# The forgetting bias of an attention stage, moved from TensorE to a broadcast by DMA and the vector engine

## The chip, the cores and the metric

One core of one Trainium2 chip runs the whole program. The metric is the device time of one execution in microseconds (us), as a median over runs. All data is float32 (f32) in memory.

## The reference, cut to what matters

The program computes two transformer blocks over 256 tokens of width 2048: a first block (modulation vectors, a Fourier mixer, a squared-relu MLP) and a second block. The second block projects the normed tokens with one wide matrix `w_in` into queries, keys, values and gates of three mixers (gated linear attention, forgetting attention "fox" with 4 heads of 128, attention to a memory with 4 heads of 128), norms and gates their outputs, multiplies by `w_out`, and ends with another MLP. The change is in the logits of the forgetting attention:

```python
c = jnp.cumsum(log_f.astype(jnp.float32), axis=-1)          # (B, 4 heads, 256)
logits = (jnp.einsum('bhqd,bhkd->bhqk', qb, kb).astype(jnp.float32) * scale
          + c[:, :, q0:q1, None] - c[:, :, None, :q1])
mask = (q0 + jnp.arange(FOX_BLOCK))[:, None] >= jnp.arange(q1)[None, :]
p = jax.nn.softmax(jnp.where(mask, logits, -jnp.inf), axis=-1)
```

## The kernel before, in words

Every large weight matrix streams from memory once, in chunks of 512 KB (two 128-row slices by 512 columns) into a ring of 8 slots of `raw`. ScalarE copies a chunk to a rounded high half `wh` (L892), VectorE subtracts to make the low half `wl` (L1224, the function `lo`), and TensorE multiplies the halves with the high and low halves of the activations in 24 (or 12 wide) matmuls a chunk. One group is 8 chunks and makes 512 output columns; the second block's input projection is the 12 groups of `WIN_GROUPS`, numbered k = 0 to 11 (k = 4, 5, 6 are the fox queries, keys and values, k = 7 the memory queries, k = 8 to 11 the gates).

Each engine runs its own instruction list in order, and semaphores tie the lists together. The attention work is placed by hand between chunks of the projection. On TensorE the loop near the end of the tensor program calls it after chunk i of group k. The ones that matter here, by (k, i): after (7, 7) the sums of squares for the head norms; after (8, 3) `att_qk("fox", ...)` (L769), the logits, which go into PSUM banks 4 to 7; after (9, 0) `att_turn` (L787), which transposes the probabilities and waits for the semaphore `fox_p`; after (9, 4) `att_pv` (L795), which waits for `fox_pt`. The same three steps of the memory attention stand after (10, 3), (11, 2) and (11, 5).

In `att_qk` a float32 matmul shows as two records in the trace. For each of 4 heads and 2 query blocks there is one 128-row matmul of queries and keys (L774). For fox two more follow into the same PSUM region: the cumulated logarithms `fc` (4 partitions, 32 to 35, by 256 tokens) as stationary operand against a one-hot column `sel` (L777, gives +c of the query), and a row of minus one `nsel` against `fc` (L779, gives -c of the key). Both have 4 rows only. `sel` and `nsel` are loaded as constants.

On VectorE group k starts with `lo_run`, the low halves of chunks 4 to 7 of group k and 0 to 3 of group k + 1, so it runs ahead of TensorE by half a group. After it, at the end of k = 7, come the head norms of the fox queries and keys (`scale_heads`, L1613), which release the logits on TensorE (`fox_qk_ready`). After the `lo_run` of k = 8 comes `soft("fox", ...)`: it waits for the logits, adds the causal mask from PSUM to `pf` (L1651), takes the maximum (L1655), lets ScalarE exponentiate (L1135), and divides (L1660), which sets `fox_p`. ScalarE then goes on with the gates of group 8 (L1147 and on), and VectorE copies the transposed probabilities to `pt` (L1692).

GpSimd's list issues side DMAs: the mask and `nsel`, the spill of `h`, the reload of the memory keys and values `mk`, `mv`, and later the reload of `h`. `fc` is ready when the scan at L1760 ends, in group 0. In this stage slots 8 to 11 of `raw` are unused.

Of the kernel before, what the change touches and what calls it, by code (L numbers as in the profile page):

```python
# [34 lines left out]
P = 128  # L35
D = 2048
S = 256
# [31 lines left out]

def program(nc, x, c, w_mod, b_mod, norm_g, w_mlp_in, w_mlp_out, fnet_w_out, mem, attn_g, w_in, gla_w2, gla_b,  # L70
            fox_b, fox_qg, fox_kg, mem_g, w_mem_kv, mem_qg, mem_kg, out_g, w_out, mlp_g, w_up, w_down,
            k_ident, k_dft, k_mask, k_nsel, k_sel, k_levels, out):
    ctx = ExitStack()
    with ctx:
        sems = {}
# [69 lines left out]
        mk = at("mk", [P, 4, S], F32, O_ACC1)  # L145
        mv = at("mv", [P, HALVES, GC], F32, O_ACC1 + 4 * KB)
        mask = at("mask", [P, HALVES, S], F32, O_SLOT)
        nsel = at("nsel", [64, 4, P], F32, O_SLOT + 2 * KB)

        ident = const("ident", [P, P], F32)  # L150
        ones = const("ones", [P, P], F32)
        vrow = const("vrow", [P, P], F32)
        vt = const("vt", [P, VROWS], F32)
        lmask = const("lmask", [P, 8, P], U8, 1)
        sel = const("sel", [64, 4], F32)
        foxb = const("foxb", [64, 1], F32)
        eps = const("eps", [P, 1], F32)
        silu32 = const("silu32", [P, KT, QP], F32)
# [7 lines left out]
        ps = ctx.enter_context(nc.psum_tensor("ps", [P, 8, 512], F32))  # L166
        mk_dram = nc.dram_tensor("mk_spill", [P, 4 * S], F32).ap()
        mv_dram = nc.dram_tensor("mv_spill", [P, HALVES * GC], F32).ap()
        h_dram = nc.dram_tensor("h_spill", [P, HALVES * D], F32).ap()

        def rows(w):
# [2 lines left out]
        def flat(ap):  # L174
            return ap.rearrange("p a b -> p (a b)")
# [175 lines left out]
        def _(pool):  # L351
# [56 lines left out]

            pool.wait_ge(sem("slot_used"), 4 + MODN)
            pool.dma_start(mask[:, :, :], k_mask.rearrange("p (a s) -> p a s", a=HALVES)).then_inc(sem("att_const"), 16)  # L410
            pool.dma_start(nsel[32:36, :, :], k_nsel.rearrange("p (a s) -> p a s", a=4)).then_inc(sem("att_const"), 16)
            pool.wait_ge(sem("h_piece"), 8)
            pool.dma_start(h_dram, flat(h[:, :, :])).then_inc(sem("h_spilled"), 16)
            pool.wait_ge(sem("la_mm"), 1)
# [3 lines left out]
            pool.wait_ge(sem("mv_spilled"), 16)  # L418
            pool.dma_start(flat(mk[:, :, :]), mk_dram).then_inc(sem("mkv_in"), 16)
            pool.dma_start(flat(mv[:, :, :]), mv_dram).then_inc(sem("mkv_in"), 16)  # L420
            pool.wait_ge(sem("mem_pv"), 1)
            pool.wait_ge(sem("h_spilled"), 16)
            pool.dma_start(flat(h[:, :, :]), h_dram).then_inc(sem("h_back"), 16)
# [3 lines left out]
        def _(pe):  # L427
# [338 lines left out]
                    last = mm(ps[:, bank + j, :], ones[:, :], flat(sq[:, 2 * j:2 * j + 2, :]), start=True, stop=True)  # L766
                last.then_inc(sem(name + "_mm"), 1)

            def att_qk(name, qq, kk, fox):  # L769
                pe.wait_ge(sem(name + "_qk_ready"), 1)  # L770
                for hd in range(4):
                    for tb in range(HALVES):
                        o = ps[:, 4 + hd, tb * S:(tb + 1) * S]
                        last = mm(o, qq[:, hd, tb * P:(tb + 1) * P], kk[:, hd, :], start=tb == 0, stop=not fox,  # L774
                                  skip_group_check=True)
                        if fox:
                            mm(o, fc[32:36, tb * P:(tb + 1) * P], sel[32:36, hd:hd + 1].to_broadcast([4, S]),  # L777
                               start=False, stop=False, skip_group_check=True)
                            last = mm(o, nsel[32:36, hd, :], fc[32:36, :], start=False, stop=True, skip_group_check=True)  # L779
                last.then_inc(sem(name + "_qk"), 1)  # L780

            def att_turn(name, pr):
# [17 lines left out]
            for k, (name, off) in enumerate(WIN_GROUPS):  # L800
                G = G_WIN + k
                bank_free(G)
                for i in range(CH):
                    if k == 0 and i % 2 == 0:
                        pe.wait_ge(sem("xt_ready"), 8 + i // 2 + 1)
                    sr = (i, CH * G + i + 1)
                    if name in ("gv", "fv"):
                        N_chunk(G, i, xt, False, *sr)
                    else:
                        T_chunk(G, i, False, *sr)  # L810
                    if (k, i) == (0, 1):
                        att_narrow()
                    if (k, i) == (0, 5):
                        att_la()
                    if 2 <= k <= 6 and i == 3:
                        att_level(2 * (k - 2))
                    if 2 <= k <= 5 and i == 6:
                        att_level(2 * (k - 2) + 1)
                    if (k, i) == (6, 6):
                        att_gla_out()  # L820
                    if (k, i) == (7, 3):
                        att_sums("o", 1, osq, 8, 4)
                    if (k, i) == (7, 7):
                        pe.wait_ge(sem("o_ln"), 1)
                        att_sums("fq", 1, fqsq, 4, 4)
                        att_sums("fk", 1, fksq, 4, 6)
                    if (k, i) == (8, 3):
                        pe.wait_ge(sem("att_const"), 32)
                        att_qk("fox", fq, fk, True)
                    if (k, i) == (9, 0):  # L830
                        att_turn("fox", pf)
                    if (k, i) == (9, 4):
                        att_pv("fox", lambda sb_, hd: fvv[:, sb_, hd * P:(hd + 1) * P])
                        att_sums("mq", 1, tmp, 4, 6)
                    if (k, i) == (9, 7):
                        att_sums("fo", 1, fosq, 4, 4)
                    if (k, i) == (10, 3):
                        pe.wait_ge(sem("mkv_in"), 32)
                        pe.wait_ge(sem("fo_ln"), 1)
                        att_qk("mem", mq, mk, False)  # L840
                    if (k, i) == (11, 2):
                        att_turn("mem", pm)
                    if (k, i) == (11, 5):
                        att_pv("mem", lambda sb_, hd: mv[:, sb_, hd * P:(hd + 1) * P])
                    if (k, i) == (11, 7):
                        att_sums("mo", 1, tmp, 4, 6)
# [30 lines left out]
        def _(act):  # L877
            A = nc.scalar.activation
            col = lambda t: t.rearrange("(a o) -> a o", o=1)
            consts = [(dft_raw[:, :, :], k_dft.rearrange("(a p) n -> p a n", p=P)),  # L880
                      (foxb[32:36, :], col(fox_b)), (sel[32:36, :], k_sel), (lmask_raw[:, :], k_levels)]
            assert len(consts) == N_CONSTS
            row_loads(act, 0)
            for dst, src in consts:
# [326 lines left out]
        def _(dve):  # L1211
# [434 lines left out]
            def soft(name, pr, masked):  # L1646
# [1 line left out]
                dve.wait_ge(sem(name + "_qk"), 1)  # L1648
                src, dst = ps[:, 4:8, :], banks(pr[:, :, :], 4)
                if masked:  # L1650
                    link(V.tensor_tensor(dst, src, flat(mask[:, :, :]).rearrange("p (o n) -> p o n", o=1)  # L1651
                                         .to_broadcast([P, 4, 2 * S]), ALU.add))
                else:
                    link(V.tensor_copy(dst, src))
                link(V.tensor_reduce(mx[:, :], pr[:, :, :], AX.X, ALU.max))  # L1655
# [42 lines left out]
            for k, (name, off) in enumerate(WIN_GROUPS):  # L1698
# [73 lines left out]
                if k == 7:  # L1772
                    dve.wait_ge(sem("fq_root"), 1)
                    dve.wait_ge(sem("fk_root"), 1)
                    link(scale_heads(fq, lambda j: v("fqg"), fqsq[:, :, :], 4))
                    scale_heads(fk, lambda j: v("fkg"), fksq[:, :, :], 4).then_inc(sem("fox_qk_ready"), 1)

            for g in range(GQ):
                G = G_WO + g
# [14 lines left out]
WIN_GROUPS = [("gq", 0), ("gk", 0), ("gv", 0), ("gv", GC), ("fq", 0), ("fk", 0), ("fv", 0), ("mq", 0),  # L1794
              ("gg", 0), ("gg", GC), ("fg", 0), ("mg", 0)]
N_ROWS = 13
N_CONSTS = 4
G1_ROWS_AT = {0: 8, 1: 12, 3: 16, 5: 24, 6: 28}
G1_AT = [(6, 7), (), (), (20, 21), (22, 23), (), (), ()]

# [5 lines left out]
def shape_constants():  # L1806
# [9 lines left out]
        "k_ident": np.eye(P, dtype=np.float32),  # L1816
        "k_dft": np.concatenate([np.cos(angle), np.sin(angle)], 1).astype(np.float32),
        "k_mask": np.concatenate(causal, 1).astype(np.float32),
        "k_nsel": np.repeat(-np.eye(4, dtype=np.float32), P, axis=1),
        "k_sel": np.eye(4, dtype=np.float32),  # L1820
        "k_levels": np.concatenate(masks, 1).astype(np.float32),
    }

# [17 lines left out]
```

## Time and profile before

| | |
|---|---|
| median of 3 runs | 2235.99 us (2235.28 to 2237.89) |
| the profiled execution | 2238.09 us, its span 2236.3 us |
| TensorE busy (PE) | 2155.4 us |
| VectorE busy (DVE) | 1317.2 us |
| ScalarE busy (ACT) | 973.7 us |
| mean granted TensorE clock | 0.977 of full |

The span is the time from the first to the last instruction on the core. A granted clock of 1.00 is TensorE's full 2.4 GHz and 0.50 is 1.2 GHz. Matmuls are pipelined, so the busy time of TensorE also counts the overlap of neighbours and is no measure of throughput; the chain that ended last, and the distance from one matmul's step in it to the next, show the pace. Idle time of an engine that nobody waits for costs nothing.

### The profile page before, as it was taken

Reading aid. Unit: us, or ns where it says so; the run is one execution under the profiler, and the core shown is the slowest. Engines: PE = TensorE matmul, PEld = TensorE weight load, DVE = VectorE, ACT = ScalarE, POOL = GpSimd, SP = SyncE. Lnnn points to the kernel's source line nnn. Section 1 sums busy time; section 2 is a strip of 40 time slices with the busy share of each in tenths; the row PEclk is TensorE's granted clock in tenths of the full one; section 3 lists DMA queues with packets and bytes.
Section 4 is the critical chain, followed back from the end, with each engine's and each line's share of the span. In section 5 each row is a group of like instructions: output and inputs, shape, how many; then the busy total and the mean of one; then the engine's idle time right before and its main releaser. Section 6 shows DMA issues by size and latency. Waiting matters only on the chain.

```text
span 2236.3 us, 31309 instructions
## 1 busy us (share of the span) xinstructions
PE 2155.4 (96%) x11753; PEld 1823.1 (82%) x11753; DVE 1317.2 (59%) x1301; ACT 973.7 (44%) x1133; POOL 45.1 (2%) x69
## 2 busy tenths in 40 slices
PE   5999988999999999997999999999999999999999
PEld 3867867888888888886979879888888888888887
DVE  3568976555655555655666546646545554655563
ACT  4244435443444444443533447744444343443342
POOL 0000000000000000000000000000000000000000
PEclk9889989999999999998999989999999999999999
DMA  9899996667666667676455435556656656656654
GB/s 389 280 403 347 391 372 194 215 216 215 206 224 207 213 210 218 205 223 203 145 164 147 136 100 145 191 186 188 189 194 189 186 192 189 187 190 193 183 192 151
DMA packets 219188, 478.98 MB, mean 214 GB/s; under 512 B 14708, under 2 KB 15084, under 8 KB 218336
## 3 DMA queue, kind: packets, MB, share of 16 engines
q1 hardware_dynamic: 211940, 450.98, 62.5%
q0 software_dynamic: 6480, 25.69, 3.6%
q8 instruction: 60, 0.98, 0.2%
q10 hardware_dynamic: 684, 1.14, 0.1%
q14 instruction: 24, 0.20, 0.0%
HBM read 472.50 MB, written 5.24 MB: 214 GB/s over the span
## 4 chain that ended last, share of the span: by engine, by line
PE 88%; DVE 5%; DMA 4%; ACT 2%; issue 1%; SPq 0%; DVEq 0%; ACTq 0%
PE ps L441 21%; PE ps L459 13%; PE ps L461 13%; PE ps L460 13%; PE ps L442 11%; PE ps L445 3%; PE ps L446 3%; PE ps L447 3%; DMA raw<-in_w_mod_dram 1%; DVE acc L1249 1%; DMA raw<-in_w_in_dram 1%; PE ps L485 1%; PE ps L507 1%; DVE wl L1224 1%; DMA slot<-in_norm_g_dram 1%
## 5 line engine op out<-in xcount | busy, mean ns | idle before, releaser
L1224 DVE TENSOR_TENSOR wl<-raw,wh 128x1024 fp32r<-128x1024 f32 x688 | 811.2, 1220 | 345.5 <-ACT wh L892 344.4
L892 ACT ACTIVATE wh<-raw 128x1024 fp32r<-128x1024 f32 x688 | 700.7, 1054 | 559.0 <-DMA raw<-in_w_down_dram 161.6
L441 PE MATMUL ps<-xt,wh 128*128 128x512 f32 x2048 | 724.8, 399 | 9.0 <-DVE wl L1224 9.0
L442 PE MATMUL ps<-xt,wl 128*128 128x256 f32 x2048 | 575.5, 281 | 0.0
L441 PEld LDWEIGHTS ps<-xt,wh 128*128 128x128 f32 x2048 | 386.2, 189 | 106.1 <-issue 10.7
L459 PE MATMUL ps<-wh,u 128*128 128x512 f32 x1152 | 449.3, 390 | 0.0
L460 PE MATMUL ps<-wl,u 128*128 128x512 f32 x1152 | 448.2, 389 | 0.0
L461 PE MATMUL ps<-wh,u 128*128 128x512 f32 x1152 | 448.2, 389 | 0.0
L442 PEld LDWEIGHTS ps<-xt,wl 128*128 128x128 f32 x2048 | 388.3, 190 | 0.3
L459 PEld LDWEIGHTS ps<-wh,u 128*128 128x128 f32 x1152 | 216.2, 188 | 45.2 <-issue 0.5
L461 PEld LDWEIGHTS ps<-wh,u 128*128 128x128 f32 x1152 | 216.2, 188 | 45.1
L460 PEld LDWEIGHTS ps<-wl,u 128*128 128x128 f32 x1152 | 216.2, 188 | 44.9 <-issue 0.5
L445 PE MATMUL ps<-xt,wh 128*128 128x256 f32 x640 | 187.6, 293 | 4.0 <-DVE wl L1224 4.0
L446 PE MATMUL ps<-xt,wh 128*128 128x256 f32 x640 | 184.2, 288 | 0.0
L447 PE MATMUL ps<-xt,wl 128*128 128x256 f32 x640 | 184.1, 288 | 0.0
L1502 DVE TENSOR_TENSOR tmp<-ps,tmp 128x1024 f32<-128x1024 f32 x32 | 39.2, 1225 | 172.7 <-ACT tmp L1067 172.7
L445 PEld LDWEIGHTS ps<-xt,wh 128*128 128x128 f32 x640 | 126.1, 197 | 9.1 <-issue 8.5
L446 PEld LDWEIGHTS ps<-xt,wh 128*128 128x128 f32 x640 | 126.1, 197 | 1.1 <-issue 1.0
L447 PEld LDWEIGHTS ps<-xt,wl 128*128 128x128 f32 x640 | 126.0, 197 | 0.0
L1067 ACT ACTIVATE tmp<-ps 128x1024 f32<-128x1024 f32 x32 | 32.9, 1027 | 201.1 <-PE ps L442 201.1
L459 PE MATMUL ps<-wh,xt 128*128 128x512 f32 x256 | 102.5, 400 | 3.6 <-DVE wl L1224 3.6
L1249 DVE SCALAR_TENSOR_TENSOR acc<-raw,siluc,acc 128x1024 f32<-128x1024 f32 x80 | 102.2, 1279 | 4.9 <-DMA raw<-in_w_mod_dram 1.7
(266 smaller groups left out, 1514.5 us busy)
## 6 DMA issues: line engine op xcount, KB each, us to landing
raw<-in_w_mod_dram SPq DMA_DIRECT2D x160, 512.0 KB, 8.0
raw<-in_w_mlp_in_dram SPq DMA_DIRECT2D x128, 512.0 KB, 3.8
raw<-in_w_mlp_out_dram SPq DMA_DIRECT2D x128, 512.0 KB, 3.9
raw<-in_w_up_dram SPq DMA_DIRECT2D x128, 512.0 KB, 3.8
raw<-in_w_down_dram SPq DMA_DIRECT2D x128, 512.0 KB, 3.7
raw<-in_w_in_dram SPq DMA_DIRECT2D x96, 512.0 KB, 3.7
raw<-in_fnet_w_out_dram SPq DMA_DIRECT2D x32, 512.0 KB, 5.6
slot<-in_w_mod_dram POOLq DMA_DIRECT2D x32, 512.0 KB, 4.6
```

Of the source, the lines that this page charges most:

```text
L441: mm(o, a, flat(xt[:, kt, :, :]), start=first, stop=end, skip_group_check=True)
L442: last = mm(o[:, 0:S], b, xt[:, kt, 0, :], start=False, stop=end, skip_group_check=True)
L445: mm(o, a, xt[:, kt, 0, :], start=first and j % 2 == 0, stop=False, skip_group_check=True)
L446: mm(o, a, xt[:, kt, 1, :], start=False, stop=False, skip_group_check=True)
L447: last = mm(o, b, xt[:, kt, 0, :], start=False, stop=end, skip_group_check=True)
L459: mm(o, hi, wh[:, i, t, :], start=kt == 0, stop=False, skip_group_check=True)
L460: mm(o, hi, wl[:, s, t, :], start=False, stop=False, skip_group_check=True)
L461: last = mm(o, lo, wh[:, i, t, :], start=False, stop=kt == KT - 1, skip_group_check=True)
L892: A(flat(wh[:, i, :, :]), raw[:, landed[0], :], ACT.Copy).then_inc(sem("w_hi"), 1)
L1224: V.tensor_tensor(flat(wl[:, s, :, :]), raw[:, s, :], flat(wh[:, i, :, :]).bitcast(F32), ALU.subtract).then_inc(sem("w_lo"), 1)
L1249: V.scalar_tensor_tensor(out=t, in0=raw[:, s, :], scalar=siluc[:, kt:kt + 1], in1=t, op0=ALU.mult, op1=ALU.add).then_inc(mod_used(mod_c(c0 ...
L1502: V.tensor_tensor(tmp[:, :, :], ps[:, b0:b0 + 4, 0:S], tmp[:, :, :], ALU.add).then_inc(sem("evacuated"), 1)
```

## The change: what it does

The 32 calls of four-row matmuls (L777, L779) go; `att_qk` keeps its 8 query-key matmuls. In their place `fc` is written to memory by GpSimd's queue, and read back twice: broadcast to all 128 partitions (`fcb`, 4 heads by 256 keys, 512 KB), and with queries on partitions (`fcq`, 128 by 8 numbers, 4 bytes each). VectorE then makes `bias` = mask + fcq - fcb in 8 instructions of 128x256 at the end of group k = 7, behind the instruction that releases the logits on TensorE and ahead of the `lo_run` of k = 8. `soft` adds `bias` where it added the mask. The constants `sel` and `nsel` and their loads go.

```diff
+        fcq = at("fcq", [P, 8], F32, O_SLOT + 3 * KB)
+        fcb = at("fcb", [P, 4, S], F32, O_RAW + RAW * 4 * KB + 4 * KB)
+        bias = at("bias", [P, 8, S], F32, O_RAW + RAW * 4 * KB + 8 * KB)
...
             pool.dma_start(flat(mv[:, :, :]), mv_dram).then_inc(sem("mkv_in"), 16)
+            pool.wait_ge(sem("fc_ready"), 1)
+            pool.dma_start(fc_dram, fc[32:36, :]).then_inc(sem("fc_out"), 16)
+            pool.wait_ge(sem("fc_out"), 16)
+            pool.dma_start(flat(fcb[:, :, :]), fc_dram.rearrange("h s -> (h s)").rearrange("(o n) -> o n", o=1)
+                           .to_broadcast([P, 4 * S])).then_inc(sem("fc_in"), 16)
+            pool.dma_start(fcq[:, :].rearrange("p (h t) -> p h t", h=4),
+                           fc_dram.rearrange("h (t p) -> p h t", p=P), allow_slow_non_contiguous=True).then_inc(sem("fc_in"), 16)
             pool.wait_ge(sem("mem_pv"), 1)
...
-                        last = mm(o, qq[:, hd, tb * P:(tb + 1) * P], kk[:, hd, :], start=tb == 0, stop=not fox,
-                                  skip_group_check=True)
-                        if fox:
-                            mm(o, fc[32:36, tb * P:(tb + 1) * P], sel[32:36, hd:hd + 1].to_broadcast([4, S]),
-                               start=False, stop=False, skip_group_check=True)
-                            last = mm(o, nsel[32:36, hd, :], fc[32:36, :], start=False, stop=True, skip_group_check=True)
+                        last = mm(ps[:, 4 + hd, tb * S:(tb + 1) * S], qq[:, hd, tb * P:(tb + 1) * P], kk[:, hd, :],
+                                  start=tb == 0, stop=True, skip_group_check=True)
...
-                    link(V.tensor_tensor(dst, src, flat(mask[:, :, :]).rearrange("p (o n) -> p o n", o=1)
-                                         .to_broadcast([P, 4, 2 * S]), ALU.add))
+                    link(V.tensor_tensor(dst, src, banks(bias[:, :, :], 4), ALU.add))
...
                     scale_heads(fk, lambda j: v("fkg"), fksq[:, :, :], 4).then_inc(sem("fox_qk_ready"), 1)
+                    dve.wait_ge(sem("att_const"), 16)
+                    dve.wait_ge(sem("fc_in"), 32)
+                    for j in range(8):
+                        last = V.scalar_tensor_tensor(out=bias[:, j, :], in0=mask[:, j % 2, :], scalar=fcq[:, j:j + 1],
+                                                      in1=fcb[:, j // 2, :], op0=ALU.add, op1=ALU.subtract)
+                    link(last)
```

## Rows read from the trace of the kernel before

**Rows 1.** The page: an engine's busy time, and shares of the chain that ended last.

```profile
PE 2155.4 (96%) x11753; PEld 1823.1 (82%) x11753; DVE 1317.2 (59%) x1301; ACT 973.7 (44%) x1133; POOL 45.1 (2%) x69
...
PE 88%; DVE 5%; DMA 4%; ACT 2%; issue 1%; SPq 0%; DVEq 0%; ACTq 0%
```

**Rows 2.** Windows: stretch, length, busy by engine, granted clock, DMA share, GB/s.

```profile
1307.65:1312.35 4.70, 4.70 (x18) 2.61 (x17) 4.70 (x5) 2.11 (x2) 0.00 (x0) 1.00 0.42 122
1312.35:1328.36 16.01, 16.01 (x32) 8.39 (x31) 2.10 (x2) 0.00 (x0) 0.00 (x0) 0.50 0.00 0
1328.36:1332.90 4.54, 4.54 (x22) 4.54 (x23) 4.47 (x2) 0.00 (x0) 0.00 (x0) 0.51 0.00 0
1332.90:1344.91 12.01, 12.01 (x103) 12.01 (x102) 2.67 (x11) 6.86 (x19) 0.00 (x0) 1.00 0.63 169
1385.24:1388.70 3.46, 3.46 (x19) 3.04 (x18) 2.74 (x3) 1.86 (x3) 0.00 (x0) 1.00 0.59 175
```

**Rows 3.** Chain that ended last, TensorE: start, length, line, records.

```profile
1307.65 0.43 PE ps L774 x2
...
1309.14 0.63 PE ps L774 x2
...
1322.05 1.15 PE ps L774 x2
...
1325.20 1.15 PE ps L774 x2
...
1327.50 0.85 PE ps L779 x2
...
1344.91 1.75 PE ps L787 x16
```

**Rows 4.** VectorE in order of time: start, length, line; idle before, releaser.

```profile
1289.18 3.26 DVE L1613 SCALAR_TENSOR_TENSOR ot<-ot,vt,osq 128x256 f32<-128x256 f32 x8 [5.28 <-ACT osq L1130]
...
1305.28 9.16 DVE L1224 TENSOR_TENSOR wl<-raw,wh 128x1024 fp32r<-128x1024 f32 x8
1328.39 2.29 DVE L1651 TENSOR_TENSOR pf<-ps,mask 128x2048 f32<-128x2048 f32 x1 [13.95 <-PE ps L779]
...
1337.56 2.19 DVE L1660 TENSOR_SCALAR pf<-pf,rs 128x256 f32<-128x256 f32 x8
...
1355.61 2.28 DVE L1692 COPY pt<-ps 128x2048 f32<-128x2048 f32 x1
```

**Rows 5.** ScalarE in order of time: the last exponential's read-out, the gate after it.

```profile
1337.11 0.19 ACT L1135 ACTIVATION_READ_ACCUMULATOR pf<-pf,nmx 128x1 f32 x1
1342.07 1.02 ACT L1147 ACTIVATE gt<-ps 128x1024 f32<-128x1024 f32 x1 [4.77 <-PE ps L447]
```

**Rows 6.** Waits from 1405 to 1412 us: total, times, longest.

```profile
PE ps L787 <- DVE pm L1660: 0.6, 1, 0.6
```

**Rows 7.** Windows: TensorE idle, or the busy stretch right after.

```profile
176.90:180.44 3.54, 0.02 (x2) 0.00 (x1) 3.47 (x11) 2.18 (x5) 0.00 (x0) 0.81 1.02 400
180.44:185.46 5.02, 5.02 (x23) 5.02 (x24) 4.92 (x9) 0.00 (x0) 0.00 (x0) 0.50 0.95 342
66.88:70.84 3.96, 0.00 (x0) 0.03 (x1) 3.78 (x4) 0.38 (x1) 0.00 (x0) 0.88 0.72 227
70.84:76.66 5.82, 5.82 (x27) 5.82 (x28) 2.93 (x3) 1.06 (x1) 0.00 (x0) 0.50 0.99 340
...
1172.14:1173.97 1.83, 0.00 (x1) 0.00 (x1) 1.29 (x2) 0.45 (x1) 0.00 (x0) 1.00 0.64 142
...
305.95:307.60 1.65, 0.00 (x1) 0.00 (x0) 0.00 (x0) 1.57 (x4) 0.00 (x0) 1.00 1.01 387
```

**Rows 8.** VectorE in order of time: the end of the scan, the copy in group 1.

```profile
1107.56 0.47 DVE L1760 TENSOR_TENSOR_SCAN fc<-ones,fc,fft 4x128 f32<-4x128 f32 x1
...
1123.98 1.22 DVE L1744 COPY kg<-ps 128x1024 f32<-128x1024 f32 x1 [5.42 <-PE ps L447]
```

**Rows 9.** DMA issues, 1000 to 1020 us: form, size, median us to landing.

```profile
wsr<-in_w_in_dram POOLq DMA_DIRECT2D x1, 128.0 KB, 6.3
```

More of the change, by code:

```diff
@@ L71, in program @@
             fox_b, fox_qg, fox_kg, mem_g, w_mem_kv, mem_qg, mem_kg, out_g, w_out, mlp_g, w_up, w_down,
-            k_ident, k_dft, k_mask, k_nsel, k_sel, k_levels, out):
+            k_ident, k_dft, k_mask, k_levels, out):
     ctx = ExitStack()
@@ L147, in program @@
         mask = at("mask", [P, HALVES, S], F32, O_SLOT)
-        nsel = at("nsel", [64, 4, P], F32, O_SLOT + 2 * KB)
+        fcq = at("fcq", [P, 8], F32, O_SLOT + 3 * KB)
+        fcb = at("fcb", [P, 4, S], F32, O_RAW + RAW * 4 * KB + 4 * KB)
+        bias = at("bias", [P, 8, S], F32, O_RAW + RAW * 4 * KB + 8 * KB)
         ident = const("ident", [P, P], F32)
@@ L154, in program @@
         lmask = const("lmask", [P, 8, P], U8, 1)
-        sel = const("sel", [64, 4], F32)
         foxb = const("foxb", [64, 1], F32)
@@ L168, in program @@
         mv_dram = nc.dram_tensor("mv_spill", [P, HALVES * GC], F32).ap()
+        fc_dram = nc.dram_tensor("fc_spill", [4, S], F32).ap()
         h_dram = nc.dram_tensor("h_spill", [P, HALVES * D], F32).ap()
@@ L410, in _ @@
             pool.dma_start(mask[:, :, :], k_mask.rearrange("p (a s) -> p a s", a=HALVES)).then_inc(sem("att_const"), 16)
-            pool.dma_start(nsel[32:36, :, :], k_nsel.rearrange("p (a s) -> p a s", a=4)).then_inc(sem("att_const"), 16)
             pool.wait_ge(sem("h_piece"), 8)
@@ L767, in att_sums, with att_qk @@
                 last.then_inc(sem(name + "_mm"), 1)
-            def att_qk(name, qq, kk, fox):
+            def att_qk(name, qq, kk):
                 pe.wait_ge(sem(name + "_qk_ready"), 1)
@@ L772, in att_qk @@
                     for tb in range(HALVES):
-                        o = ps[:, 4 + hd, tb * S:(tb + 1) * S]
-                        last = mm(o, qq[:, hd, tb * P:(tb + 1) * P], kk[:, hd, :], start=tb == 0, stop=not fox,
-                                  skip_group_check=True)
-                        if fox:
-                            mm(o, fc[32:36, tb * P:(tb + 1) * P], sel[32:36, hd:hd + 1].to_broadcast([4, S]),
-                               start=False, stop=False, skip_group_check=True)
-                            last = mm(o, nsel[32:36, hd, :], fc[32:36, :], start=False, stop=True, skip_group_check=True)
+                        last = mm(ps[:, 4 + hd, tb * S:(tb + 1) * S], qq[:, hd, tb * P:(tb + 1) * P], kk[:, hd, :],
+                                  start=tb == 0, stop=True, skip_group_check=True)
                 last.then_inc(sem(name + "_qk"), 1)
@@ L827, in _ @@
                     if (k, i) == (8, 3):
-                        pe.wait_ge(sem("att_const"), 32)
-                        att_qk("fox", fq, fk, True)
+                        att_qk("fox", fq, fk)
                     if (k, i) == (9, 0):
@@ L839, in _ @@
                         pe.wait_ge(sem("fo_ln"), 1)
-                        att_qk("mem", mq, mk, False)
+                        att_qk("mem", mq, mk)
                     if (k, i) == (11, 2):
@@ L880, in _ @@
             consts = [(dft_raw[:, :, :], k_dft.rearrange("(a p) n -> p a n", p=P)),
-                      (foxb[32:36, :], col(fox_b)), (sel[32:36, :], k_sel), (lmask_raw[:, :], k_levels)]
+                      (foxb[32:36, :], col(fox_b)), (lmask_raw[:, :], k_levels)]
             assert len(consts) == N_CONSTS
@@ L1796 @@
 N_ROWS = 13
-N_CONSTS = 4
+N_CONSTS = 3
 G1_ROWS_AT = {0: 8, 1: 12, 3: 16, 5: 24, 6: 28}
@@ L1818, in shape_constants @@
         "k_mask": np.concatenate(causal, 1).astype(np.float32),
-        "k_nsel": np.repeat(-np.eye(4, dtype=np.float32), P, axis=1),
-        "k_sel": np.eye(4, dtype=np.float32),
         "k_levels": np.concatenate(masks, 1).astype(np.float32),
```

## The prediction

> **What bounds the kernel now.** I read the page first. TensorE is busy 96% of the span and 88% of the chain that ended last is TensorE's, while the vector engine is busy 59% [rows 1]. A cut of TensorE work is worth its length, as long as nobody else becomes late. So the second view is the chain around the changed block, and the third is the windows cut at its borders.
>
> The fox logits take TensorE from 1307.65 us to 1328.36 (the last piece of L779 starts at 1327.50 and takes 0.85) [rows 3], so 20.7 us. The memory attention's logits are the same 8 matmuls without the 32 four-row ones and take 3.46 us at full clock [rows 2]. The reader should see two causes in the 20.7. First, the round of three matmuls repeats every 1.49 us at the start (1307.65 to 1309.14), where a lone query-key pair would take 3.46 / 8 = 0.43. Second, from the fourth round on it repeats every 3.15 us (1322.05 to 1325.20) [rows 3]: the granted clock is 1.00 up to 1312.35 and 0.50 from there, that is 1.2 instead of 2.4 GHz [rows 2]. The engine had issued matmuls without a gap since the block began, two thirds of them with 4 rows. The clock stays low for 4.54 us after the block: five chunks of 24 matmuls stand between the block and the transpose, 21 of these 120 steps take 4.54 us and the 99 others 12.01, which is 0.12 each [rows 2]. All 120 at full clock would be 14.4 us. So the block costs 20.7 + 2.0 (4.54 less 21 x 0.12 = 2.5), against 3.46 without the four-row matmuls: **19.3 us** less for TensorE alone.
>
> A rule of the Trainium skill speaks against that size. "TensorE: Matmul & The Clock Gate", in the part on LDWEIGHTS of "Part 2: What happens when you issue a matmul", says that time goes by columns and the row count does not matter. By that the 48 records of 256 columns would take 48 / 16 x 3.46 = 10.4 us and the cut would be 6.9 us; the trace has 20.7, so it does not agree, at either clock. The sum goes by the trace.
>
> **The vector engine's side.** Before, it had nothing to do for 13.95 us ahead of the mask addition, waiting for L779 [rows 4]. That slack goes, and what stands behind it must be walked through. Times are those of the profiled execution; everything up to 1305.28 stays.
> - At 1305.28 the release of the logits has been given, and `lo_run` of k = 8 starts, 8 instructions in 9.16 us [rows 4]. The change puts its 8 bias instructions ahead. The same operation on 128x256 with the same operand kinds took 3.26 us for 8 (L1613) [rows 4]; this one I take at 3.3. Nothing hides it, since the engine has no gap from there to the softmax. `lo_run` runs from 1308.6 to 1317.7.
> - Queued behind them on the engine are the low halves that TensorE wants. The first, chunk (8, 4), is ready at 1308.6 + 1.2 = 1309.8. TensorE wants it when the logits end, at 1307.65 + 3.46 = 1311.1. It is in time by 1.3 us, and the others gain on it, for a chunk takes 24 x 0.12 = 2.9 us on TensorE and 1.15 on the vector engine.
> - The softmax starts at 1317.7 instead of 1328.39. From the start of the addition to the end of the division it took 1337.56 + 2.19 - 1328.39 = 11.36 us [rows 4], ScalarE's part included; the addition of `bias` has the shape and the PSUM source of that of the mask, so I take it the same. `fox_p` comes at 1329.1.
> - TensorE does five chunks between the logits and the transpose: 1311.1 + 14.4, with 0.3 for the switch of matmul kinds, is 1325.8. Then **it waits 3.3 us**, for `fox_p`. The transpose starts at 1329.15 instead of 1344.91 [rows 3]: **15.8 us** earlier. The other 3.5 of the 19.3 are the bias instructions, come back as a wait. That such a chain can be late shows in the memory attention, where the transpose has two chunks (5.8 us) more of cover and TensorE still waits 0.6 us [rows 6].
> - The wait has a price in clock. After idle stretches of 3.54 and 3.96 us TensorE's clock had fallen inside the stretch (means of 0.81 and 0.88), and it stood at 0.50 for 5.02 and 5.82 us of work afterwards; an idle of 1.83 us did nothing [rows 7]. At 305.95, 1.65 us of idle showed 1.00. A wait of 3.3 us is nearest to the first. Priced: the transpose, 1.75 us at full clock [rows 3], takes twice that, as the round of the logits did (3.15 against 1.49), +1.75; the other 1.5 us of a 5.0 us slow stretch lose 1.5 x (1 - 0.120 / 0.216) = 0.65, with 4.54 / 21 = 0.216 for the slow step [rows 2]. Together **+2.4 us**. Bounds: 0 if the clock holds; 2.75 for a stretch of 5.8 us.
> - What is late next: `att_pv` wants `pt`. ScalarE ends its exponentials 8.9 us after the addition starts (1337.3) and then waited 4.77 us for group 8 to end before the gate at 1342.07 [rows 5]. Now it goes straight on, at 1317.7 + 8.9 = 1326.7, 15.4 earlier. The copy to `pt` ended at 1357.9 [rows 4], so now at 1342.5. TensorE gets there at 1329.15 + 1.75 + 4 chunks = 1342.4, or 1344.8 with the slow clock. So 0 to 0.1 us. The rest of the program follows TensorE's pace as it did, and shifts as a whole.
>
> **The DMAs.** `fc` is ready at 1108.0 [rows 8], and `fcq`, `fcb` are needed at 1305.3, 197 us later. GpSimd's queue has nothing behind them but the reload of `h`, which waits for the memory attention (after 1420). The only price is in the way of the weight ring at 1110 to 1120. There the vector engine waits 5.42 us before its copy at 1123.98 [rows 8], so weights that are late by less cost nothing. `fcb` is 512 KB, like one weight chunk. `fcq` is 1024 runs of 4 bytes; the nearest row is `wsr`, 2048 runs of 64 bytes, landed in 6.3 us among other loads [rows 9]. I take 0, with 3 us as the upper bound (half of `wsr`'s time with the ring standing still). The two small constant loads that go were never waited for: between 0 and 0.3 us of gain, taken as 0.
>
> **The sum.** 19.3 - 3.5 - 2.4 = 13.4 us less. Against the profiled execution, 2238.09 - 13.4 = 2224.7; that execution was 2.1 us over the median of 2235.99, so the time on the median is **2222.6 us**.
>
> **The rivals.**
> 1. The wait comes, but the clock holds, as in the idle stretches of 1.83 and 1.65 us: 15.8 less, **2220.2**. For it: 3.3 us is shorter than both stretches that ended slow. A variant gives the same time: if the clock fell at 1312 from whatever cause, and not from the four-row matmuls, TensorE would come to the transpose 2 us later and the wait would swallow it. Against the variant: the memory logits kept 1.00 [rows 2]. Chance 0.25.
> 2. The clock falls and stays low for long, since transposes of 128 columns may do less to lift it than full matmuls. With 10 us low the loss is 1.75 + 6.5 x 0.44 = 4.6: **2224.8**. Chance 0.08.
> 3. The cover holds: the softmax is not what TensorE waits for, and all 19.3 come: **2216.7**. Against it stands the length of the chain above, each link with a row. Chance 0.03.
> 4. The gain is eaten to less than 4.5 us: bias instructions at 1.2 us each instead of 0.41 (the copy of four times the elements took 1.22 [rows 8]) add 8 x 0.8 = 6.3 us of wait, and up to 4 more if the low halves then come late too: 13.4 - 6.3 = 7.1 down to 3, **2229 to 2233**. Chance 0.04.
> 5. Slower than before: the 1024 four-byte runs choke the 16 DMA engines at 1110 to 1120. It decides from the point where the ring stands still for more than the 5.42 us of slack plus the 13.4 gained, so 19 us, and gives over **2236**. That is 0.3 us per run on one engine (19 x 16 / 1024); `wsr`, with twice the runs, took 6.3 us in all, under 0.05 each. Chance 0.02. The Trainium skill, "DMA: Bandwidth & Descriptors", "Specifications", has a read-modify-write below 512 bytes a run, which speaks for such a price but gives no number for it here.
>
> **How the numbers follow.** The forecast has 0.58. The range goes from 2218 (rival 1 with 2 us for what the execution-to-execution spread of 2.6 us allows) to 2228.5 (rival 2, plus 3 us of DMA, plus 0.7), which leaves out rivals 3, 5 and most of 4. Within 0.2% is within 4.5 us of 2235.99, about what a measurement of this kernel can tell from no change: chance 0.04, from rival 4 at its dearest and mishaps in the DMA; slower 0.02; faster 0.94.
>
> **What would show it.** Right: the logits as 16 records of L774's form in about 3.5 us at clock 1.00; 8 bias instructions of about 0.41 us; no idle of the vector engine before the addition; TensorE waiting about 3.3 us at the transpose for L1660's counterpart, and 0.50 in the 5 us after it; the transpose 21.5 us after the first logit matmul, where it was 37.3 (1307.65 to 1344.91) [rows 3]. Wrong: an idle vector engine before the addition (cover longer than I think), a wait at `fc_in`, ScalarE waiting for weights at 1110 to 1125, or a new wait at `att_pv`.

## The result, and the profile after

The changed kernel takes 2222.5 us (median of 4 runs, 2221.3 to 2224.6), where the kernel before takes 2236.94 (4 runs, 2235.28 to 2241.51): a ratio of 0.9938, with a 95% interval of 0.9925 to 0.9952. That is 14.4 us less. The profiled execution took 2221.78 us, its span 2219.8.

One number ahead of the prediction, and in it, wants a correction: the change removes 16 calls of four-row matmuls, not 32. Each call is two records, so there are 32 records, and every duration in the prediction was taken by records or by pieces of the chain.

The page of the changed kernel, busy times and shares of the chain that ended last (compare [rows 1]):

```profile
PE 2136.3 (96%) x11721; PEld 1811.5 (82%) x11721; DVE 1320.7 (59%) x1309; ACT 973.4 (44%) x1133; POOL 46.5 (2%) x71
...
PE 86%; DVE 6%; DMA 4%; ACT 3%; issue 1%; SPq 0%; DVEq 0%; ACTq 0%
```

TensorE has 32 records less, the vector engine 8 instructions more, and the vector engine's share of the chain has risen. Why it has is in the chain itself, from the changed kernel's trace (start, length, line, records):

```profile
1302.92 3.18 DVE bias L1781 x8
...
1306.12 9.17 DVE wl L1226 x8
1315.30 2.21 DVE pf L1653
...
1320.06 4.06 ACT pf L1137 x16
...
1324.38 2.20 DVE pf L1661 x8
...
1326.63 2.59 PE ps L790 x16
...
1341.66 3.46 PE ps L798 x16
```

From 1302.9 to 1326.6 the chain no longer runs through TensorE: bias instructions, low halves, softmax, then the transposes (L790). Before, TensorE's logits stood there [rows 3]. The vector engine's row for the addition has no idle time in it, where it had 13.95 us [rows 4]:

```profile
1315.22 2.28 DVE L1653 TENSOR_TENSOR pf<-ps,bias 128x2048 f32<-128x2048 f32 x1
```

In group 1, where the new DMAs run, the last low half and the copy behind it, first before, then after:

```profile
1117.34 1.23 DVE L1224 TENSOR_TENSOR wl<-raw,wh 128x1024 fp32r<-128x1024 f32 x1 [1.23 <-ACT wh L892]
```

```profile
1117.31 1.23 DVE L1226 TENSOR_TENSOR wl<-raw,wh 128x1024 fp32r<-128x1024 f32 x1 [3.63 <-ACT wh L894]
1121.56 1.23 DVE L1745 COPY kg<-ps 128x1024 f32<-128x1024 f32 x1 [3.02 <-PE ps L455]
```

The idle time ahead of the low half grew by 2.4 us and that ahead of the copy shrank by as much, from 5.42 us [rows 8]. The two together stay at 6.65 us. The low half waits for ScalarE, whose wait for this chunk of weights grew from 1.76 to 4.20 us.

Windows of the changed kernel: the logits, the wait, the stretch after it (columns as in [rows 2]), and the wait by name:

```profile
1305.20:1308.66 3.46, 3.46 (x19) 3.04 (x18) 3.42 (x6) 1.06 (x1) 0.00 (x0) 1.00 0.61 171
1323.05:1326.63 3.58, 0.01 (x2) 0.01 (x1) 2.39 (x9) 3.55 (x8) 0.00 (x0) 1.00 0.60 171
1326.63:1331.20 4.57, 4.57 (x27) 4.57 (x28) 2.97 (x3) 4.52 (x5) 0.00 (x0) 0.63 0.00 0
```

```profile
PE ps L790 <- DVE pf L1661: 3.6, 1, 3.6
```

The logits take 3.46 us at full clock. TensorE then waits 3.58 us for the probabilities. The clock holds in the wait and falls behind it: a mean of 0.63 over the 4.57 us that follow, at levels of 1.00 and 0.50.

A caution on comparing the two profiled executions. Their spans differ by 16.5 us. The end of the fox norms, which nothing of the change precedes but the DMAs and the two constant loads that went, stands at 1305.28 before (start of the next row in [rows 4]) and at 1302.84 after, 2.44 us apart. The same spot of the program comes between 1300.7 and 1306.2 us in the profiles of this study. So I measure from there. The kernel before has its product of probabilities and values at this place of its chain:

```profile
1358.17 3.50 PE ps L795 x16
```

That is 52.9 us behind the norms before, and 38.8 after (1341.66). It makes 14.1 us of gain by the change itself, and 2.4 us that were there when the norms ended.

### The profile page after: what moved, and what is told of

It is laid out like the page before. It is cut to its first block, busy times and chain, and to the rows that moved or that the text cites. A ratio compares the mean times of both kernels' runs of the same rounds, so it can differ in the third digit from the quotient of the medians.

```text
span 2219.8 us, 31255 instructions
## 1 busy us (share of the span) xinstructions
PE 2136.3 (96%) x11721; PEld 1811.5 (82%) x11721; DVE 1320.7 (59%) x1309; ACT 973.4 (44%) x1133; POOL 46.5 (2%) x71
## 4 chain that ended last, share of the span: by engine, by line
PE 86%; DVE 6%; DMA 4%; ACT 3%; issue 1%; SPq 0%; DVEq 0%; ACTq 0%
PE ps L449 21%; PE ps L467 13%; PE ps L468 13%; PE ps L469 13%; PE ps L450 11%; PE ps L453 3%; PE ps L455 3%; PE ps L454 3%; DMA raw<-in_w_mod_dram 1%; DVE acc L1251 1%; DVE wl L1226 1%; PE ps L493 1%; PE ps L515 1%; DMA raw<-in_w_in_dram 1%; DMA slot<-in_norm_g_dram 1%
```

## The experiments

Twelve runs follow, two of them repeats of a kernel, in three groups, each on one chip together with the kernel before (its medians there: 2236.2, 2236.5, 2236.3 us). The 95% intervals of the ratios reach about 3 us to either side, so the claims below lean on the traces, and the times check them. Where a distance "from the norms" is given, it runs from the end of the fox norms, as above.

**The bias instructions earlier.** They move into the vector engine's idle time ahead of the norms' roots.

```diff
                 if k == 7:
+                    dve.wait_ge(sem("att_const"), 16)
+                    dve.wait_ge(sem("fc_in"), 32)
+                    for j in range(8):
+                        last = V.scalar_tensor_tensor(out=bias[:, j, :], in0=mask[:, j % 2, :], scalar=fcq[:, j:j + 1],
+                                                      in1=fcb[:, j // 2, :], op0=ALU.add, op1=ALU.subtract)
+                    link(last)
                     dve.wait_ge(sem("fq_root"), 1)
                     dve.wait_ge(sem("fk_root"), 1)
                     link(scale_heads(fq, lambda j: v("fqg"), fqsq[:, :, :], 4))
                     scale_heads(fk, lambda j: v("fkg"), fksq[:, :, :], 4).then_inc(sem("fox_qk_ready"), 1)
-                    dve.wait_ge(sem("att_const"), 16)
-                    dve.wait_ge(sem("fc_in"), 32)
-                    for j in range(8):
...
-                    link(last)
```

> The changed kernel with its 8 bias instructions moved ahead of the wait for the norms' roots at the end of group 7, where the vector engine idles 7.9 us. Theory (the bias instructions stand on the chain to the softmax, and the 3.6 us wait that they make lowers TensorE's clock): the probabilities come 3.3 us earlier, TensorE waits about 0.3 us at the fox transpose, the clock stays at 1.00, and 3.3 + 1.8 = 5.1 us go: about 2217.4 us where the changed kernel has 2222.5. Rival (something else sets the wait, weights or ScalarE): the wait stays over 3 us and the time within 1 us of 2222.5.

Measured: 2219.35 us, ratio 0.9927 (0.9914 to 0.994). First the vector engine's row and the transposes and product in the chain, then TensorE's wait, all of this kernel:

```profile
1293.49 3.25 DVE L1777 SCALAR_TENSOR_TENSOR bias<-mask,fcq,fcb 128x256 f32<-128x256 f32 x8
```

```profile
1325.34 1.97 PE ps L790 x16
1338.82 3.49 PE ps L798 x16
```

```profile
PE ps L790 <- DVE pf L1661: 0.3, 1, 0.3
```

The wait falls from 3.6 to 0.3 us, as the theory has it. The product starts 34.0 us from the norms (1338.82 less 1304.85), 4.8 earlier than in the changed kernel's profile. The rival is out. The median fell by less than the expected 5.1; it was run again on a third chip:

> The kernel with the bias instructions ahead of the norms' wait once more, as footing for the next three on one chip. Theory: 2219.4 us, as on the first chip.

Measured: 2217.63 us, ratio 0.9916 (0.9902 to 0.9929), the product 34.0 us from the norms again.

**No bias at all.** The kernel leaves out the bias: no spill, no reloads, no bias instructions.

```diff
-            pool.wait_ge(sem("fc_ready"), 1)
-            pool.dma_start(fc_dram, fc[32:36, :]).then_inc(sem("fc_out"), 16)
...
-                    dve.wait_ge(sem("fc_in"), 32)
-                    for j in range(8):
...
-                    link(V.tensor_tensor(dst, src, banks(bias[:, :, :], 4), ALU.add))
+                    link(V.tensor_tensor(dst, src, flat(mask[:, :, :]).rearrange("p (o n) -> p o n", o=1)
+                                         .to_broadcast([P, 4, 2 * S]), ALU.add))
```

> The changed kernel without the forgetting bias at all: no spill of the cumulated logarithms, no reloads, no bias instructions, the mask alone is added; the output lacks the bias. Theory (the DMAs are free, the bias instructions cost only by their place): the same as the kernel with the bias instructions moved ahead, about 2217.4 us. Rival (the broadcast and the four-byte reload hold up the weight ring): over 1 us faster than that kernel, and ScalarE waits less for weights between 1105 and 1125 us.

Measured: 2218.91 us, ratio 0.992 (0.9906 to 0.9935). The chain of this kernel:

```profile
1326.41 1.97 PE ps L783 x16
...
1339.89 3.49 PE ps L791 x16
```

The product stands 34.0 us from the norms (1339.89 less 1305.91), like the kernel with the early bias instructions, and the times agree. One sign of the rival did show: without the DMAs ScalarE waits 1.78 us for the weights near 1117 us, where it waits 4.24 with them in the kernel with the early instructions. The time doesn't show it, because the vector engine's idle time behind takes it in. So the whole machinery of the bias, 3 DMAs and 8 instructions, costs nothing once the instructions sit in a gap, and its 3.3 us plus what the clock takes where the change puts them.

**128 rows in place of 4,** on the kernel before. Each four-row matmul becomes one more query-key matmul, so the bias is left out and the logits are wrong.

```diff
-                            mm(o, fc[32:36, tb * P:(tb + 1) * P], sel[32:36, hd:hd + 1].to_broadcast([4, S]),
+                            mm(o, qq[:, hd, tb * P:(tb + 1) * P], kk[:, hd, :],
                                start=False, stop=False, skip_group_check=True)
-                            last = mm(o, nsel[32:36, hd, :], fc[32:36, :], start=False, stop=True, skip_group_check=True)
+                            last = mm(o, qq[:, hd, tb * P:(tb + 1) * P], kk[:, hd, :], start=False, stop=True, skip_group_check=True)
```

> The kernel before with each of its 32 four-row matmuls replaced by one more 128-row query-key matmul into the same place (the output is not the reference's; the bias is left out). Theory (four rows lower the clock and break the pace): 48 records at 0.216 us, 10.4 us for the block, clock 1.00 through it and after it, about 12.3 us less than before: 2224.6 where before has 2236.9. Rival (the number of rows does not matter; any f32 block of this length lowers the clock): the block takes 20 us and the time is that of before.

Measured: 2224.73 us, ratio 0.9944 (0.993 to 0.9958). Chain and window of the block:

```profile
1307.96 0.43 PE ps L774 x2
1308.40 0.43 PE ps L777 x2
```

```profile
1307.96:1318.32 10.36, 10.36 (x51) 9.12 (x50) 6.80 (x6) 2.11 (x2) 0.00 (x0) 1.00 0.19 58
```

The block of 24 matmuls, now all with 128 rows, takes 10.4 us, where it took 20.7 with 16 of them at four rows [rows 3], and the clock stays at 1.00. The rival is out: a block of this length doesn't lower the clock by itself.

**32 rows in place of 4,** in the same place and order, the bias left out and the logits wrong (`qq[32:64, ...]`, `kk[32:64, ...]` in the lines above).

> The kernel before with its four-row matmuls replaced by matmuls of 32 rows of the queries and keys (partitions 32 to 63), in the old order; the bias is left out and the output is not the reference's. Theory (few rows are the cause, of the pace and of the clock): 32 rows behave nearly as 4 do, rounds of 1.5 us and a fall of the clock, the time within 3 us of before. Rival (only the very few rows count, or the operands' kind): rounds of 1.3 us and a clock at 1.00, as with 128 rows, 2224.7.

Measured: 2226.95 us, ratio 0.9962 (0.9949 to 0.9975). Both expectations missed a half. Chain and window:

```profile
1306.37 0.62 PE ps L777 x2
1306.99 0.43 PE ps L779 x2
1307.42 0.63 PE ps L774 x2
```

```profile
1305.93:1319.22 13.29, 13.29 (x50) 7.50 (x48) 6.80 (x6) 2.11 (x2) 0.00 (x0) 1.00 0.15 44
```

The pieces have the slow rhythm 0.62, 0.43, 0.63 of the four-row kernel (a round of 1.69), but the clock never falls. So the two costs are two things. The rhythm comes with the alternation of 128-row and short matmuls, at 4 rows and at 32 alike: 13.3 less 10.4 = 2.9 us. The clock falls with 4 rows and not with 32. The time agrees: 9.5 us under before, where the block is 7.4 us shorter and the 2.0 us of slow clock behind it are gone.

**The same four-row matmuls, grouped:** first the 8 query-key calls, then the 16 four-row calls.

```diff
+                for hd in range(4 if fox else 0):
+                    for tb in range(HALVES):
+                        o = ps[:, 4 + hd, tb * S:(tb + 1) * S]
+                        mm(o, fc[32:36, tb * P:(tb + 1) * P], sel[32:36, hd:hd + 1].to_broadcast([4, S]),
+                           start=False, stop=False, skip_group_check=True)
+                        last = mm(o, nsel[32:36, hd, :], fc[32:36, :], start=False, stop=True, skip_group_check=True)
```

> The kernel before with its matmuls in another order: first the 8 query-key matmuls, then all the four-row matmuls together; same work, same output. Theory (two causes: the switch between 128-row and four-row matmuls keeps the weight load from running ahead, and few rows lower the clock): no more 0.63 us pieces, one record each 0.216 us at full clock, but the clock still falls some 5 us into the block and the rest goes at 0.43: the block takes about 15.7 us where it took 20.7, and the time is 5 us under before, 2231. Rival (the alternation itself lowers the clock): the clock stays at 1.00, block 10.4 us, 12 us under before: 2224.

Measured: 2229.7 us (10 runs, 2224.9 to 2235.3), ratio 0.9974 (0.9962 to 0.9987), with 2227.09 for the profiled execution. Chain and windows:

```profile
1304.05 3.46 PE ps L774 x16
1307.50 0.63 PE ps L779 x2
1308.13 0.43 PE ps L781 x2
...
1312.61 0.85 PE ps L781 x2
```

```profile
1304.05:1312.20 8.15, 8.15 (x38) 6.78 (x38) 6.79 (x6) 2.11 (x2) 0.00 (x0) 1.00 0.26 72
1312.20:1322.50 10.30, 10.30 (x39) 8.81 (x38) 4.75 (x3) 0.73 (x3) 0.00 (x0) 0.50 0.01 2
```

One 0.63 remains, at the one switch; every other piece is 0.43 until the clock falls, 8.2 us into the block, 4.7 us into its four-row part. Before, it fell 4.7 us into a block that alternates from the start, 4.3 after its first four-row matmul [rows 2, 3]. The block takes 12.8 us. With no alternation left the clock falls still, so the alternation isn't its cause. What stays untested is whether the number of rows does it or what the rows hold: the four-row matmuls read the cumulated logarithms with a one-hot column or with rows of minus one, and their 32-row and 128-row substitutes read queries and keys. Four rows of queries and keys were not run. I expected the fall 5 us into the block, that is, earlier; hence 12.8 and not 15.7 in this execution. The spread of the runs (10.4 us, against 2 to 8 in the other kernels) fits a fall that comes at varying times, but only one execution was profiled.

**The transposes one chunk later,** in the changed kernel: `if (k, i) == (9, 1)` for `(9, 0)`.

> The changed kernel with the fox transpose one chunk later on TensorE, after (9, 1). Theory (the wait is a lack of cover, and its clock price goes with it): TensorE waits 0.7 us, clock 1.00, 2.9 + 1.8 = 4.7 us less: about 2217.8 us. Rival (the wait moves to the next step, the product of probabilities and values after (9, 4), whose operand the vector engine copies after the transpose): the time stays within 1 us of 2222.5.

Measured: 2222.84 us, ratio 0.9941 (0.9928 to 0.9954): the rival. One of its 6 runs took 9809 us, which nothing on record explains. It is in that median and not in the ratio; the median of the other five is 2222.31. TensorE's waits, and the window behind the one of 2.7 us:

```profile
PE ps L798 <- DVE pt L1693: 4.0, 2, 2.7
PE ps L790 <- DVE pf L1661: 0.7, 1, 0.7
```

```profile
1338.60:1345.00 6.40, 6.38 (x19) 4.89 (x20) 6.40 (x6) 2.52 (x3) 0.00 (x0) 0.73 0.07 26
```

(The 4.0 counts also the wait of about 1.4 us of the memory attention, which is in every profile but the last.) The clock fell behind this wait too, 1.4 us into the product. The transposes wait 0.7 us as expected, and the product 2.7: its operand comes from ScalarE's gate steps and the vector engine's copy, which run at their own pace from the end of the exponentials. Moving the transposes doesn't move that. My prediction had this number: it put the copy at 0 to 0.1 us behind TensorE, and I did not carry it into this expectation.

**The changed kernel again, with and without filling the wait.** In the second, 28 matmuls of full rows stand in the wait ahead of the transposes.

```diff
                     if (k, i) == (9, 0):
+                        pe.wait_ge(sem("fox_max"), 1)
+                        for n in range(28):
+                            mm(ps[:, 4, 0:S], xt[:, 0, 0, 0:P], xt[:, 0, 0, :], start=True, stop=True, skip_group_check=True)
                         att_turn("fox", pf)
```

> The changed kernel itself, on one chip with the next three, as their footing. All theories: 2222.5 us, 13 to 14 us under before.

> The changed kernel with 28 idle-filling matmuls (256 columns, high halves, into PSUM bank 4, which the transposes then overwrite) in TensorE's wait before the fox transpose; they wait for the softmax's maximum, so that the logits have been read. Theory (the idle lowers the clock, which costs 1.6 us): the clock stays at 1.00, transpose and the four chunks after it run at full pace, 1.6 us less than the changed kernel: 2220.9. Rival (the stretch after the transpose is slow for another reason, such as the f32 transposes themselves): the clock falls as before, and the time is that of the changed kernel or up to 0.5 us more.

Measured: 2222.17 us, ratio 0.9936 (0.9922 to 0.995), and 2221.45 us, ratio 0.9932 (0.9919 to 0.9946). The windows of the first, wait and after it, and where its product starts:

```profile
1323.10:1326.78 3.68, 0.12 (x2) 0.01 (x1) 2.40 (x9) 3.65 (x9) 0.00 (x0) 1.00 0.60 174
1326.78:1331.35 4.57, 4.57 (x40) 4.57 (x41) 2.97 (x3) 4.52 (x5) 0.00 (x0) 1.00 0.00 0
```

```profile
1340.25 3.49 PE ps L798 x16
```

The window after the wait, of the kernel with the filling:

```profile
1327.60:1341.10 13.50, 13.49 (x113) 13.49 (x114) 10.88 (x9) 11.84 (x12) 0.00 (x0) 1.00 0.41 112
```

The same kernel, the same wait of 3.6 us, and this time the clock held without any filling. From the start of the transposes to the product it takes 13.5 us here (1326.78 to 1340.25), where it took 15.0 in the first profile (1326.63 to 1341.66): the price of the fall, when it comes, is **1.6 us**. The filling gained 0.7 us in the median, within the scatter. As the clock held without it, this pair doesn't decide between its two expectations, and how often the clock falls isn't settled by it. Both traces of the filled and the unfilled kernel have the same distance to the product.

**The bias instructions twice,** in their place, the second time over the first.

> The changed kernel with the 8 bias instructions done twice in their place (same output). Theory (they stand one for one on the chain to the transposes, and a wait of this length always lowers the clock): TensorE waits 6.9 us at the fox transpose instead of 3.6, the clock falls in it, and the time is 3.3 us over the changed kernel where that one's clock fell too, 4.9 over where it held: 2225.5 to 2227. Rival (slack further on takes it back): under 1.5 us over 2222.2.

Measured: 2227.91 us, ratio 0.9963 (0.995 to 0.9976). TensorE's waits, the longer one being the later, then its clock around the earlier wait (1313 to 1319 us) and, in the last window, behind the later one (columns as in [rows 2]):

```profile
PE ps L790 <- DVE pf L1661: 3.1, 1, 3.1
PE ps L453 <- DVE wl L1226: 2.0, 1, 2.0
```

```profile
1313.00:1314.00 1.00, 0.00 (x0) 0.00 (x0) 1.00 (x2) 0.24 (x1) 0.00 (x0) 1.00 0.00 0
1314.00:1315.00 1.00, 1.00 (x7) 1.00 (x8) 1.00 (x1) 0.00 (x0) 0.00 (x0) 0.79 0.00 0
1315.00:1316.00 1.00, 1.00 (x6) 1.00 (x6) 1.00 (x2) 0.00 (x0) 0.00 (x0) 0.50 0.00 0
...
1317.00:1318.00 1.00, 1.00 (x7) 1.00 (x7) 1.00 (x2) 0.00 (x0) 0.00 (x0) 0.50 0.00 0
1318.00:1319.00 1.00, 1.00 (x10) 1.00 (x10) 1.00 (x2) 0.00 (x0) 0.00 (x0) 1.00 0.00 0
...
1333.00:1337.00 4.00, 3.77 (x33) 3.77 (x34) 2.34 (x3) 3.95 (x5) 0.00 (x0) 1.00 0.06 21
```

The 3.3 us go on the path one for one: the transposes start 3.3 us later from the norms (27.1 against 23.8), which rules out slack further on. I expected one wait of 6.9. There are two: the low half of chunk (8, 4), for which the prediction had counted 1.3 us of slack, is now late by 2.0 = 3.3 - 1.3. After that short wait the clock is at 0.50 for 3.4 us, at a loss of 3.4 x 0.44 = 1.5, which the second wait takes in: 2.0 + 1.5 + 3.1 = 6.6 of the 6.9. The second wait, longer than the first, leaves the clock at 1.00. That a wait of this length always lowers the clock, as I had assumed, is refuted. The median is 1 us above the range that I gave.

**The four-byte reload five times,** into four more buffers that nobody reads.

```diff
-            pool.dma_start(fcq[:, :].rearrange("p (h t) -> p h t", h=4),
+            for t in (fcq, *fcx):
+                pool.dma_start(t[:, :].rearrange("p (h t) -> p h t", h=4),
...
```

> The changed kernel with the four-byte reload done five times at once, into four more small buffers that nobody reads. In the profiles one set of reloads took the vector engine's idle time before its copy of group 1 from 5.4 to 3.0 us. Theory (1024 runs of 4 bytes hold the 16 DMA engines for under 1 us): the idle time falls by up to 1 us for each extra reload and stays at or over 0, and the time rises by under 1 us on 2222.2. Rival (the four-byte runs are what cost the 2.4 us): four more cost 9.6 us, of which the 3.0 us of idle time hide a part: about 6.6 us more, 2228.8.

Measured: 2221.55 us, ratio 0.9938 (0.9923 to 0.9954). DMA issues between 1100 and 1135 us, the vector engine's copy of group 1, and the window from the start of the fox transposes:

```profile
fcb<-fc_spill POOLq DMA_DIRECT2D x1, 512.0 KB, 5.1
fcx<-fc_spill POOLq DMA_DIRECT2D x4, 4.0 KB, 6.4
...
fcq<-fc_spill POOLq DMA_DIRECT2D x1, 4.0 KB, 5.9
```

```profile
1119.39 1.23 DVE L1747 COPY kg<-ps 128x1024 f32<-128x1024 f32 x1 [2.08 <-PE ps L457]
```

```profile
1324.54:1329.00 4.46, 4.46 (x25) 4.46 (x26) 2.86 (x3) 4.41 (x5) 0.00 (x0) 0.62 0.00 0
```

Four more reloads took the idle time from 3.0 to 2.1 us, 0.2 each, and no time in the median. The eight profiles with one set of reloads have 2.7 to 3.4 us there, the five without any 5.4, and this one is the only one with five sets, so 0.2 is an estimate, between 0.15 and 0.3. By it the 1024 four-byte runs are about a tenth of the 2.4 us by which the change shortened that idle time. The rest is left to the 512 KB broadcast and the spill ahead of it, which were not run apart.

**One more step,** with the early bias instructions: the memory attention's product after (11, 6).

> The kernel with the early bias instructions, and the memory attention's product of probabilities and values one chunk later, after (11, 6), where TensorE waits 1.4 us for its operand in every profile. Theory: that wait goes, 1.4 us less than the kernel with the early bias instructions: 2218.0. Rival (the sums of squares after (11, 7) then wait for the product's norm instead): no gain.

Measured: 2217.72 us, ratio 0.9916 (0.9903 to 0.993), against 2217.63 for the kernel with the early bias instructions alone. TensorE's waits in the attention stage are now these two, where `PE ps L798 <- DVE pt L1693: 1.4` stood with them:

```profile
PE ps L790 <- DVE pm L1661: 0.6, 1, 0.6
PE ps L790 <- DVE pf L1661: 0.3, 1, 0.3
```

The wait has gone, no other has come for it, and the next stage's first reduction (L1580) starts 151.1 us behind the memory logits, against 152.4 in the profile of the kernel without this step: 1.3 us earlier, near the 1.4 expected. The medians don't show it: 5 runs each, scattered over 4.8 and 3.7 us. Whether it gains time stays open.

Of the kernels that keep the bias, those with the early bias instructions have the lowest medians: 2217.6 and 2219.4 us on two chips, 3 to 5 us below the changed kernel (2217.7 with the later product).

## Why the prediction was right, step by step

The forecast was 2222.6 us; 2222.5 were measured, and 2222.17 when the changed kernel ran again in the experiments. The mechanism was right; that the two agree to 0.1 us is luck. The gain was forecast at 13.4 us and came out as 14.4, and the median of the kernel before rose by 0.95 us with its fourth run (2235.99 to 2236.94), which hides the difference. Step by step:

- **19.3 us for TensorE alone.** Right: with the bias early or absent, the product stands 18.9 us earlier from the norms than before (34.0 against 52.9), with 0.3 us of wait left. Its causes are now told apart. Of the block's 20.7 us, 3.5 are the logits, 6.9 the added matmuls at full pace (10.4 with 128 rows), 2.9 the alternation (13.3 with 32 rows), and the other 7.4 the clock, with 2.0 more behind the block. The prediction held the four-row matmuls responsible for the clock with no more than coincidence to show; the 32-row, the 128-row and the grouped kernel show that they are, though not whether by their four rows or by what those hold. The prediction misread one row: the round of three matmuls takes 1.49 us only the first time, and 1.69 from the second on (1309.14 to 1310.83), so the slow round of 3.15 is 1.86 times as long, and not twice. The Trainium skill's rule that the row count does not matter ("TensorE: Matmul & The Clock Gate", Part 2, on LDWEIGHTS) is stated there of the weight load. Carried over to the matmuls, as the prediction did, it gives the first two terms, 10.4 us, and neither of the other two.
- **3.5 us back as a wait.** The bias instructions took 3.25 us, `lo_run` ended where forecast (1315.22, plus the 2.44 us by which this profile is ahead: 1317.66 against 1317.7), the wait was 3.58 for 3.3, the transposes came 21.4 us after the first logit for 21.5. The wait is longer by the 0.3 us that the prediction had allowed, without a row, for the switch of matmul kinds: from the end of the logits to the wait it is 14.4 us (1308.66 to 1323.05), the five chunks alone. With the instructions earlier or absent the wait fell by 3.3 us; with them doubled the transposes came 3.3 us later.
- **2.4 us for the clock.** This is the mis-sized term. It was priced as a fall inside the wait with 5.0 us of slow work. The fall came 1.2 us after the wait in one profile, with about 3.4 us slow (0.63 over 4.57 us), and cost 1.6. In another it didn't come at all, and in a third, the one with five reloads, it came 0.9 us after the wait and left a mean of 0.62 over 4.46 us. With the clock held the gain is 15.6 us in the trace, with the fall 14.1. So the first rival (clock holds, 2220.2) isn't refuted: the kernel does both, by execution. How often it does either isn't known. The rival's variant is out: the clock stayed at 1.00 without the four-row matmuls, and TensorE did not come to the transposes 2 us later. The second rival, 10 us of slow clock, is out too.
- **0 to 0.1 us at the product.** Right: with the clock held, the copy ends at 1339.96 (1337.68 + 2.28, second profile of the changed kernel) and the product starts at 1340.25. That link bound the kernel with the later transposes.
- **The DMAs at 0.** Right in effect, though not free of delay: ScalarE's longer wait for weights, 4.20 us where it was 1.76, is one of the signs that the prediction named as wrong. The delay of 2.4 us stayed inside the 5.42 us of cover, and inside the bound of 3, so nothing of it reached the time. The prediction put the risk on the wrong DMA: a reload of 1024 four-byte runs is worth about 0.2 us of it.

The fourth rival fell with the row of the bias instructions, 3.25 us for all 8, and the one on the slower side with the five reloads. Why the two profiled executions differ by a further 2.4 us ahead of the norms isn't known. Of these, 2.2 us are there already at ScalarE's first copy to `x1t` (300.49 before, 298.31 after), and this spot scatters: it starts between 295.4 and 300.1 us in profiles of kernels that are the same up to there.

## What to carry to other kernels

A matmul with a handful of rows can cost far more than one with 128 rows and as many columns: look at the granted clock in and behind a block of them, and at whether they alternate with full ones. When a long stretch goes from one engine, walk the other engine's instruction list from the last point that stays, with every instruction that the change adds, because what had waited for the stretch is now the chain. An instruction that another engine will wait for belongs in a gap ahead of that chain; the same eight instructions cost nothing in one place and 3.3 to 4.8 us in the other.

## What the runs showed of the hardware that was not expected

- TensorE's clock fell from 1.00 to 0.50 while it issued matmuls without a gap, when some had 4 rows (4.3 and 4.7 us after the first of them, in two orders), and stayed at 1.00 for 13.3 us at the same uneven rhythm with matmuls of 32 rows, of other operands, in their place.
- A switch between 128-row and short f32 matmuls added 0.2 us to a piece of 0.43, at 4 and at 32 rows alike.
- The length of an idle stretch did not decide about the clock: 2.0 us of it were followed by 0.50, while 3.1 us in the same execution and 3.68 us in another were not; 3.58 us were followed by 0.50 in one execution of the very same kernel. In the four profiles with such a fall it came 0.6, 0.9, 1.2 and 1.4 us into the new work, not in the wait.
- 1024 runs of 4 bytes, written to 128 partitions, landed in 5.9 us and held up the stream of weights by about 0.2 us (an estimate, from one profile with five such reloads: 3.0 less 2.1 us over four).
